# Hybrid encoder, tail of the expert mixer: pair 15's h turned and copied earlier, its down product in two halves with two token groups between

## The reference, cut to what matters

```python
    for gi in range(N_GROUPS):
        h = jax.nn.silu(jnp.einsum('td,edf->tef', xt, w_gate[gi])) * jnp.einsum('td,edf->tef', xt, w_up[gi])
        out = out + jnp.einsum('tef,efd->td', h * combine[:, gi, :, None], w_down[gi])
...
        x = x + hier_moe(hn, router_group_w[l], router_group_b[l], router_expert_w[l],
                         router_expert_b[l], expert_w_gate[l], expert_w_up[l], expert_w_down[l])
    return rms_norm(x, norm_final)
```

## Time and profile before

| | |
|---|---|
| median of 3 runs | 611.15 us |
| the runs | 611.15, 798.07, 611.04 us |
| profiled execution, its own time | 610.19 us |
| its span, first to last instruction | 608.4 us |
| PE busy | 573.6 us (94%) |
| DVE busy | 256.6 us (42%) |
| ACT busy | 212.5 us (35%) |
| mean granted TensorE clock | 0.997 of full speed |

### The profile page before, as it was taken

How to read it: one execution, slowest core, us unless ns; L and a number is a source line. 1 busy time by engine, 2 the same in 40 slices (tenths; PEclk the granted TensorE clock), 3 DMA queues, 4 the chain that set the end, 5 groups by cost and what they waited for, 6 DMA issues and landing times.

```text
span 608.4 us, 8621 instructions
## 1 busy us (share of the span) xinstructions
PE 573.6 (94%) x3429; PEld 436.8 (72%) x3430; DVE 256.6 (42%) x558; ACT 212.5 (35%) x412; POOL 58.4 (10%) x103
## 2 busy tenths in 40 slices
PE   4999999999999999999999998999999998877796
PEld 3789989888788888888888875666666765443452
DVE  2647477646535666533372475112111211102255
ACT  5446367555786623422242241111111111111114
POOL 3000000001000001100000012022112211113001
PEclk9999999999999999999999999999999999999998
DMA  7476021722231222197789575999999999999995
GB/s 253 92 259 202 16 72 43 254 93 70 69 100 42 67 71 70 36 343 281 292 310 403 237 277 226 347 424 423 423 423 426 421 423 424 424 425 424 426 420 211
DMA packets 58697, 155.76 MB, mean 256 GB/s; under 512 B 8204, under 2 KB 38308, under 8 KB 46496
## 3 DMA queue, kind: packets, MB, share of 16 engines
q1 hardware_dynamic: 53920, 145.74, 62.6%
q0 software_dynamic: 4720, 9.45, 4.1%
q10 hardware_dynamic: 16, 0.00, 0.0%
HBM read 147.31 MB, written 15.75 MB: 268 GB/s over the span
## 4 chain that ended last, share of the span: by engine, by line
PE 80%; SPq 7%; DMA 7%; DVE 3%; ACT 1%; issue 1%; POOL 1%; DVEq 0%; POOLq 0%; ACTq 0%
PE mid_rows L763 19%; PE last_rows L763 18%; PE bank L1161 12%; PE bank L763 7%; SPq L518 7%; DMA slot2e<-expert_w_up 5%; PE mid_rows L1182 5%; PE bank L756 5%; PE bank L1237 2%; PE mid_rows L858 2%; PE mid_rows L1257 1%; DMA x_in<-x 1%; PE bank L1264 1%; PE bank L836 1%; PE bank L1031 1%
## 5 line engine op out<-in xcount | busy, mean ns | idle before, releaser
L1780 DVE TENSOR_TENSOR w_low<-w,w_high 128x1024 fp32r<-128x1024 f32 x32 | 39.2, 1225 | 78.6 <-ACT w_high L1417 78.6
L1161 PE MATMUL bank<-slots,xgT 128*64 128x256 f32 x544 | 62.1, 381 | 3.9 <-DMA slots<-expert_w_up 3.5
L1161 PEld LDWEIGHTS bank<-slots,xgT 128*64 128x64 f32 x544 | 43.8, 137 | 21.7 <-DMA slots<-expert_w_up 5.2
L1417 ACT ACTIVATE w_high<-w 128x1024 fp32r<-128x1024 f32 x32 | 33.7, 1054 | 48.6 <-PE last_rows L763 48.6
L2135 DVE TENSOR_SCALAR y<-mid_rows,slot_weights 128x512 f32<-128x512 f32 x14 | 10.5, 751 | 89.6 <-PE mid_rows L1182 89.6
L1592 ACT ACTIVATE y<-mid_rows,slot_weights 128x512 f32<-128x512 f32 x14 | 9.6, 687 | 85.9 <-PE mid_rows L1182 63.1
L1750 DVE CUSTOM_DVE_ANT_0 s_sb<-bank,bias,sink 128x256 f32<-128x256 f32 (+1 forms) x32 | 17.6, 549 | 29.2 <-PE bank L837 29.1
L1586 ACT ACTIVATE h_silu<-bank 128x256 f32<-128x256 f32 x14 | 5.4, 385 | 67.9 <-PE bank L1161 67.9
L763 PE MATMUL mid_rows<-x_high,w_high 128*128 128x512 f32 x72 | 28.5, 396 | 0.0
L1182 PE MATMUL mid_rows<-slots,hT 128*64 128x512 f32 x112 | 25.4, 593 | 2.9 <-issue 2.9
L763 PE MATMUL mid_rows<-x_high,w_low 128*128 128x512 f32 x72 | 28.1, 390 | 0.0
(11 more groups left out here) (407 smaller groups left out, 1334.6 us busy)
## 6 DMA issues: line engine op xcount, KB each, us to landing
slots<-expert_w_gate SPq DMA_DIRECT2D x18, 1024.0 KB, 9.5
slots<-expert_w_up SPq DMA_DIRECT2D x18, 1024.0 KB, 10.6
slots<-expert_w_down SPq DMA_DIRECT2D x16, 1024.0 KB, 24.7
slot2b<-expert_w_down SPq DMA_DIRECT2D x11, 1024.0 KB, 28.6
w<-w_in SPq DMA_DIRECT2D x16, 512.0 KB, 3.7
w<-w_in SPq DMA_DIRECT2D x8, 840.0 KB, 4.7
slot2b<-expert_w_gate SPq DMA_DIRECT2D x6, 1024.0 KB, 27.9
slot2b<-expert_w_up SPq DMA_DIRECT2D x5, 1024.0 KB, 25.3
```

The lines of the kernel that those rows point to most:

```text
L1161: ins = mm(bank[2][e * SLOTS:(e + 1) * SLOTS, m * FE:(m + 1) * FE], xgT[:, c, e * SLOTS:(e + 1) * SLOTS], gu[m][e][:, c], start=(c == 0), ...
L1417: A(wh2[:, u % 2, :], raw2[:, u % 2, :], ACT.Copy).then_inc(s["hi_done"], 1)
L1780: V.tensor_tensor(wl2[:, u % 2, :], raw2[:, u % 2, :], wh2[:, u % 2, :].bitcast(F32), ALU.subtract).then_inc(s["lo_done"], 1)
```

## The change

Three things move. On TensorE, `last_turn_h(1)` goes ahead of group (0, 1, 3). `last_down` now does one half `f` for each call; for pair 14 the two halves still follow each other, for pair 15 the first half stands directly behind group (0, 1, 3) and the second half behind groups (0, 1, 1) and (0, 1, 2). On VectorE, `last_turned(1)` goes ahead of additions 3 and 4.

```diff
-            def last_down(i):
+            def last_down(i, f):
                 own, k, loads = weights_of(LAST + i)
                 _, dn = slot_views(own)
                 pe.wait_ge(s["lhT_done"], i + 1)
                 pe.wait_ge(m_in[k][2], loads(2))
-                for f in range(2):
-                    for j in range(2):
-                        for e in range(2):
-                            ins = mm(bank[4 + f][e * SLOTS:(e + 1) * SLOTS, :], hT[:, j, e * SLOTS:(e + 1) * SLOTS],
-                                     dn[e][:, j, f * 512:(f + 1) * 512], start=(j == 0), stop=(j == 1), skip_group_check=True)
-                    ins.then_inc(s["ldn_done"], 1)
+                for j in range(2):
+                    for e in range(2):
+                        ins = mm(bank[4 + f][e * SLOTS:(e + 1) * SLOTS, :], hT[:, j, e * SLOTS:(e + 1) * SLOTS],
+                                 dn[e][:, j, f * 512:(f + 1) * 512], start=(j == 0), stop=(j == 1), skip_group_check=True)
+                ins.then_inc(s["ldn_done"], 1)
...
-            last_down(0)
+            for f in range(2):
+                last_down(0, f)
...
             to_tokens(0, 1, 0, 1, True).then_inc(s["comb_done"], 1)
+            last_turn_h(1)
             to_tokens(0, 1, 3, 7, False)
-            last_turn_h(1)
+            last_down(1, 0)
             pe.wait_ge(s["f_acc"], 3)
             to_tokens(0, 1, 1, 0, True).then_inc(s["comb_done"], 1)
             pe.wait_ge(s["f_acc"], 4)
             to_tokens(0, 1, 2, 1, True).then_inc(s["comb_done"], 1)
-            last_down(1)
+            last_down(1, 1)
...
             last_hidden(1)
+            last_turned(1)
             accumulate(3, 2, 0, 0)
             accumulate(4, 0, 1, 1)
-            last_turned(1)
             accumulate(5, 1, 1, 0)
```

## The result

The changed kernel takes 612.88 us in the median of 8 runs (611.71 to 613.48), the kernel before 610.94 in the same comparison. The ratio is 1.0033 with a 95% interval of 1.0022 to 1.0045, that is 2.0 us slower (1.3 to 2.7); one run of the kernel before, 798.07 us, is left out of the ratio. The profiled execution took 613.48 us with a span of 611.4.

A forecast was written before the change was run, and what follows sets the result against it. TensorE's queue was taken to bound the end, with no slack before VectorE's low half. Products only reordered, the wait there costs 1.6 us: 611.15 + 1.6 = 612.8, own range 612.4 to 613.2, overall 611.2 to 614.0.

The forecast's parts named there:

- Turn, first half, groups: TensorE: early turn costs nothing, pair 15's first half down product starts at 588.04, the groups at 589.92, ending at 591.12.
- What is late: VectorE: additions 5 and 6 at 590.69, add_row(0) 592.08, last_low(1, 0) 593.23; TensorE's next product at 594.13, losing 1.63 us.
- the extra change of shapes alone: TensorE, 64 to 128 columns: without the VectorE wait, the product after the second half comes at about 592.9, 0.39 later.
- Nothing catches up: Behind 594.1 the order is unchanged and nothing else falls late, so the 1.6 us pass to the end unchanged.
- The overlap on VectorE: last_low(1, 0) starts 0.08 before its predecessor's recorded end; the skill's rule, taken literally, would make the loss 1.8 instead of 1.6.
- No VectorE wait: Rival: last_low(1, 0) comes in time, only the extra change of shapes remains, +0.39, total 611.5; chance 0.10.
- Faster: Rival: the early half down product takes all gaps off TensorE and no wait comes, gain 0.46, total 610.7; chance 0.03.
- Late down weights: Rival: pair 15's down weights land beyond the 0.83 margin, each us adding one for one, 613.8 with 1 over; chance 0.05.
- The clock: Rival: 1.2 us idle on TensorE drops the last 10 us of products to 1.2 GHz, total 622.8; chance 0.02.
- one twice as long was harmless: Argument against the clock falling: 2.78 us idle on TensorE ahead of 567.81 left the granted clock at 1.00.
- The total: Whole kernel: median 611.15 plus the 1.6 us loss gives 612.8.

The follow-up runs named there:

- f0: The changed kernel measured once more without an edit: 612.39 us, ratio 1.0029 to the kernel before.
- e1: Changed kernel with VectorE's last_low(1, 0) ahead of add_row(0) and last_low(1, 1) ahead of add_row(1): 611.59 us, ratio 1.0018 to the kernel before.
- g1: Changed kernel with pair 15's whole down product ahead of groups (0, 1, 1) and (0, 1, 2), and VectorE's low halves earlier: 612.61 us, ratio 1.0030.
- f6: Changed kernel with VectorE's add_row(1) also ahead of last_low(1, 0): 614.07 us in a single run.
- f5: Changed kernel with transposes and copy of pair 15's h back at their old places, only the down product's split left: 612.94 us, single run.
- e3: Kernel before with VectorE's add_row(1) moved ahead of last_low(1, 0), nothing moved on TensorE: 611.91 us, ratio 1.0015.
- e2: Kernel before with only the early transposes and copy of pair 15's h, down product whole at its old place: 613.37 us, ratio 1.0034.

## Why the prediction was right, point by point

*Turn, first half, groups.* From the first group, the prediction has the first half at 2.00 us (588.04), the groups behind it at 3.88 and their end at 5.08. The profile has 2.05, 3.91 and, for the second half, 5.04. Additions 3 and 4 were hidden as said. Of the copy about 0.1 us was not, although the prediction says that the earlier turn costs nothing on TensorE; its sum starts the first half from the copy's end, so the total has it. One row is read under a wrong name: 590.67 is the start of the second half's first product, whose weights were loaded one step ahead, at 590.24 by the trace. The 1.77 us and the end at 592.39 hold for the products.

*What is late.* Relative to the first group, additions 5 and 6 were forecast at 4.65 and came at 4.68, `add_row(0)` at 6.04 and came at 6.07, `last_low(1, 0)` at 7.19 and came at 7.21. TensorE's product was forecast at 8.09 and came at 8.11. The loss in the stretch was forecast as 1.63 and is 1.65 and, in the second profile (f0), 1.62.

*Split of the loss.* The prediction puts the extra change of shapes alone at 0.39, that is what is left if the low half comes in time. e1 measured 0.42. Part of this agreement is luck. The sum leaves out the 0.11 between the second half and the spread that it has at the first half, and starts the second half 0.07 us later than e1 did (5.08 against 5.01), since it takes the modelled end of a product for the start of the next. And by g1 only about 0.24 of the 0.42 is the change of shapes. It puts the idle time at some 1.2; it is 1.13 in both profiles of the changed kernel.

*Behind the spread.* "Nothing catches up" holds: 15.88 us to the end against 15.90.

*The overlap on VectorE.* In the changed kernel `last_low(1, 0)` starts at 594.62, 0.09 before the recorded end of `add_row(0)` (593.48 + 1.23), so the row's hand-over was the right one. The sentence of the Trainium skill that the prediction sets against it (VectorE: DVE Perf Modes, The DRAIN you can't avoid) is not the whole of that section: it also says that a next operation that isn't held starts earlier. Read whole, it doesn't contradict the row.

*The rivals.* No VectorE wait: fell to the 1.13 us row. Faster: fell, since the gaps on TensorE were not there to be had. Late down weights: in no profile did the down product wait for them. The margin of 0.83 was 0.86 in f6 and in g1. In the execution of the changed kernel they had landed at 587.05, 2.4 us ahead of 589.46.

*The clock.* Here a step was wrong, though the total didn't rest on it. The prediction says of the idle time of 2.78 us ahead of 567.81 that "one twice as long was harmless". It rested on one execution. In 4 of 13 profiles the products behind this idle time ran in part at the lower level, and the way to the first group took 1.3 to 1.6 us more than the 18.23 of the kernel before, in variants of the kernel before too. The Trainium skill (TensorE: Matmul & The Clock Gate, Why this matters for your kernels) warns of idle gaps between bursts, but of longer ones than these. The profiles agree that a gap can bring the lower clock back, and differ in that 1.96 us was enough in f5; the measurement decides. The idle time that the change itself added, 1.13 us, never did this: the granted clock behind it was 1.00 in all four profiles with such a wait, also behind the 2.38 us of f6.

*The total.* 612.8 was forecast and 612.88 measured. That is closer than the working deserves, and partly luck: the base it started from, 611.15, was the median of three, 0.2 us above the 610.94 of eight, and the measured difference is 1.8 to 2.0 where 1.6 was forecast. The two errors cancel. The interval of the difference is more than 1 us wide, so the stretch, and not the median, is what bears the mechanism out; whether the 0.2 to 0.4 us beyond it are real stays open.

## What to carry to other kernels

When work is moved up on one engine, ask first what feeds on the work that it overtakes. The first half of the product came 0.8 us earlier and its result lay unused for 2.5 us, because the engine that had to take it was in order, and stood behind additions that the move had pushed back by 2.3 us (from 2.39 to 4.68 behind the first group). On this stretch, where TensorE's queue is full, none of the reorderings tried won anything: the added change between products of 64 and 128 columns cost about 0.24 us, and a queue that meets its reader to within 0.05 us before the change has no room for one more item ahead of it (0.64 us lost in e3, 1.2 more in f6).

## What the runs showed of the hardware

Of ten executions with the same instructions up to there, four showed a fall of the granted clock to 0.50 around the end of an idle time of 1.96 to 2.72 us on TensorE, and six, with 1.35 to 2.78 us, showed 1.00 throughout. The fall doesn't always stand at the idle time itself: in e2 it came before the products began again, in e3 only about 1 us after. That moves the time by about 1.5 us, nearly as much as the change under study. A single profile can't price an idle time of this length in either direction. The two sides of a comparison also can't be subtracted by their spans: 3.0 us of difference in one pair of profiles, 1.5 in the other, and 1.65 and 1.62 in the stretch that the change touches.
